# The RMS norm roots of a two-network fp32 kernel: tokens on partitions, one-column sums, and a root spread by TensorE

## What is computed

```
def rmsnorm(x, g):
    return x * rsqrt(mean(x*x, axis=-1) + 1e-6) * g

# network 1, for each of 2 layers; x is 512 tokens x 1024
h = rmsnorm(x, norm_mix_pre)
... h @ w_in: pooling, gated convolution, dilated attention, merged by gates
x = x + rmsnorm(merged @ w_out, norm_mix_post)
h = rmsnorm(x, norm_mem_pre)
x = x + rmsnorm(memory_cross_attention(h, rmsnorm(mem), ...), norm_mem_post)
h = rmsnorm(x, norm_ffn_pre)
x = x + rmsnorm(ffn(h), norm_ffn_post)

# network 2, for each of 2 layers; 512 tokens and, in layer 0, 256 context tokens
h = modulate(rms_norm(x, g), shift, scale)
x = x + gate * rms_norm(mixer(h) @ w_out, g)
h = modulate(rms_norm(x, g), shift, scale)
x = x + gate * rms_norm(mlp(h), g)
```

## Time and profile before

| | |
|---|---|
| time, median of 3 runs | 3810.55 us (3807.89 to 3810.62) |
| span of the profiled execution | 3805.3 us, 5.2 us less than that median, which is what lies around the span |
| PE busy, DVE busy, ACT busy, POOL busy | 95%, 53%, 40%, 6% of the span |
| the chain that ended last | PE 82%, DVE 8%, ACT 6%, issue 2% |
| ACT_TABLE_LOAD of line 1366 | 26, 33.4 us in all |

### The profile page before, as it was taken

One profiled execution on the slowest core, in us unless ns is written; L12 is line 12 of the kernel. 1 busy time (PEld: TensorE's weight loads), 2 busy tenths in 40 slices (PEclk: granted clock), 3 DMA queues, 4 the chain that ended last, 5 costly groups with the idle time before them and its releaser, 6 DMA issues.

```text
span 3805.3 us, 52598 instructions
## 1 busy us (share of the span) xinstructions
PE 3605.1 (95%) x19348; PEld 2957.6 (78%) x19348; DVE 2018.6 (53%) x3396; ACT 1504.8 (40%) x2302; POOL 241.7 (6%) x384
## 2 busy tenths in 40 slices
PE   8999989999999998899999988899999998899998
PEld 6788876887787887688778776788888777667886
DVE  4634466777764455577774465442333444644344
ACT  4344354332324534533235366432122334743233
POOL 0000000001000000000000052000000002610000
PEclk9999999999999999999999999999999999999999
DMA  3222322446332233144551102111211122112322
GB/s 132 93 72 95 98 80 83 147 140 195 119 99 78 71 106 108 42 149 139 191 164 56 50 2 42 45 50 61 66 61 61 55 63 58 31 45 78 99 94 83
DMA packets 113071, 333.14 MB, mean 88 GB/s; under 512 B 32792, under 2 KB 33688, under 8 KB 112408
## 3 DMA queue, kind: packets, MB, share of 16 engines
q1 hardware_dynamic: 74112, 265.23, 21.6%
q0 software_dynamic: 14400, 52.44, 4.3%
q10 hardware_dynamic: 24408, 13.46, 1.6%
HBM read 328.99 MB, written 6.00 MB: 88 GB/s over the span
## 4 chain that ended last, share of the span: by engine, by line
PE 82%; DVE 8%; ACT 6%; issue 2%; DVEq 1%; POOL 0%; ACTq 0%; DMA 0%; POOLq 0%; SPq 0%
PE PS L602 14%; PE PS L604 13%; PE PS L603 13%; PE PS L984 10%; PE PS L985 10%; PE PS L987 10%; PE PS L1112 1%; PE PS L677 1%; PE PS L771 1%; ACT PB L1675 1%; ACT FULL_P L1675 1%; ACT L1366 1%; PE PS L783 1%; DVE HVAL L1958 1%; DVE Y L2371 1%
## 5 line engine op out<-in xcount | busy, mean ns | idle before, releaser
L1914 DVE TENSOR_TENSOR WL<-RAW,WH 128x1024 fp32r<-128x1024 f32 x494 | 604.5, 1224 | 573.5 <-ACT WH L1330 568.2
L1330 ACT ACTIVATE WH<-RAW 128x1024 fp32r<-128x1024 f32 x494 | 521.2, 1055 | 636.3 <-PE PS L987 350.2
L602 PE MATMUL PS<-HHI,WH 128*128 128x512 f32 x1632 | 651.2, 399 | 24.5 <-DVE HLO L1951 16.2
L604 PE MATMUL PS<-HHI,WL 128*128 128x512 f32 x1632 | 639.9, 392 | 0.0
L603 PE MATMUL PS<-HLO,WH 128*128 128x512 f32 x1632 | 638.0, 391 | 0.0
L984 PE MATMUL PS<-H2HI,WH 128*128 128x512 f32 (+1 forms) x1336 | 470.0, 352 | 0.0
L985 PE MATMUL PS<-H2LO,WH 128*128 128x512 f32 (+1 forms) x1336 | 446.6, 351 | 0.0
L602 PEld LDWEIGHTS PS<-HHI,WH 128*128 128x128 f32 x1632 | 307.4, 188 | 105.3 <-issue 19.7
L987 PE MATMUL PS<-H2HI,WL 128*128 128x512 f32 (+1 forms) x1336 | 387.4, 350 | 0.0
L604 PEld LDWEIGHTS PS<-HHI,WL 128*128 128x128 f32 x1632 | 307.1, 188 | 70.5
L603 PEld LDWEIGHTS PS<-HLO,WH 128*128 128x128 f32 x1632 | 307.3, 188 | 64.3 <-issue 0.5
(11 more groups left out here) (353 smaller groups left out, 5737.0 us busy)
## 6 DMA issues: line engine op xcount, KB each, us to landing
RAW<-in_stream SPq DMA_DIRECT2D x494, 512.0 KB, 3.6
MODW<-in_modw POOLq DMA_DIRECT2D x96, 512.0 KB, 4.6
bias_rows<-in_rpb ACTq DMA_DIRECT2D x8, 476.2 KB, 6.7
X<-in_x SPq DMA_DIRECT2D x4, 512.0 KB, 5.5
MEM<-in_mem ACTq DMA_DIRECT2D x2, 1024.0 KB, 4.9
CROW<-in_crow POOLq DMA_DIRECT2D x4, 512.0 KB, 4.7
BIAS<-bias_rows ACTq DMA_DIRECT2D x8, 224.0 KB, 5.0
GRID<-bias_rows ACTq DMA_DIRECT2D x8, 224.0 KB, 4.6
```

The costliest lines, as they stand in the source:

```text
L602: nc.tensor.matmul(out, WH[:, slot, b * P:(b + 1) * P], hi, start=start, stop=False)
L604: return nc.tensor.matmul(out, WL[:, slot, b * P:(b + 1) * P], hi, start=False, stop=stop)
L1330: A(WH[:, d, :], RAW[:, s, :], ACT.Copy).then_inc(high_split, 1)
L1914: TT(WL[:, d, :], RAW[:, s, :], WH[:, d, :].bitcast(F32), ALU.subtract).then_inc(split_ready, 1)
```

## The change

RS moves from SBUF to PSUM banks 6 and 7. The sums are taken with the roles of the operands turned: a 128 x 128 block of the squares is the stationary matrix and one column of ones the moving one (`token_sums`), so a set of 512 tokens is four matmuls of one column, and the sums of 128 tokens come to lie on 128 partitions, 4 or 6 columns in all (TOKEN_SUMS, in bank 5). ACT takes a square root of 128 x 4 or 128 x 6 (ROOT), DVE its reciprocal (ROOT_INVERSE), and TensorE multiplies that column, repeated 128 times as the stationary matrix, by the identity (`roots_spread`), which puts the root of each token on all partitions of RS. Four matmuls of `keep_clock` go ahead of these. `statistics` sums ACC with seven squares in it and then the eighth square by itself. The last `split_high` and `split_low` of a stage move behind the square root and behind the residual. In ACT's evictions the square comes before the copy, and its end is signalled by itself. The table of the square root is loaded ahead of the squares. `keep_clock` writes bank 2 and not 5, and the identity is brought in by ACT's queue at the start. The diff, cut to its core:

```diff
@@ -123,6 +123,8 @@
+        ROOT = place("ROOT", [P, 8])
+        ROOT_INVERSE = place("ROOT_INVERSE", [P, 8])
...
@@ -137,7 +139,6 @@
-        RS = place("RS", [P, TA], at=S0 + 3 * TA)
...
@@ -254,6 +255,8 @@
+        RS = FLAT[:, 6 * T:6 * T + TA]
+        TOKEN_SUMS = FLAT[:, 5 * T + TC:5 * T + TC + 8]
...
@@ -472,7 +475,6 @@
-            sp.dma_start(IDENT[:], consts[:, 0:P]).then_inc(consts_in, 16)
...
@@ -654,17 +656,38 @@
-                    nc.tensor.matmul(bank(5, P), ONES[:], IDENT[:], start=True, stop=True)
-
-            def statistics(n):
+                    nc.tensor.matmul(bank(2, P), ONES[:], IDENT[:], start=True, stop=True)
+
+            def token_sums(src, n, start, stop):
+
+                for b in range(n // P):
+                    last = nc.tensor.matmul(TOKEN_SUMS[:, b:b + 1], src[:, b * P:(b + 1) * P], ONES[:, 0:1], start=start and b == 0, stop=stop,
+                                            skip_group_check=True)
+                return last
+
+            def roots_spread(n):
+
+                keep_clock(4)
+                m.add("inverted")
+                pe.wait_ge(root_inverted, m.at("inverted"))
+                for b in range(n // P):
+                    last = nc.tensor.matmul(RS[:, b * P:(b + 1) * P], ROOT_INVERSE[:, b:b + 1].to_broadcast([P, P]), IDENT[:], start=True, stop=True,
+                                            skip_group_check=True)
+                last.then_inc(root_ready, 1)
+
+            def statistics(n, last_square=None):
...
-                m.add("sqt", KB - 1)
+                m.add("sqt", KB - 2)
...
-                for c0 in range(0, n, T):
-                    c1 = min(c0 + T, n)
-                    last = nc.tensor.matmul(FLAT[:, 6 * T + c0:6 * T + c1], ONES[:], ACC[:, c0:c1], start=True, stop=True)
-                last.then_inc(stat_done, 1)
+                token_sums(ACC[:], n, True, False)
+                if last_square is None:
+                    m.add("sq", KB)
+                    pe.wait_ge(sq_ready, m.at("sq"))
+                else:
+                    pe.wait_ge(y_squared, last_square)
+                token_sums(SQ[:, 1, :], n, False, True).then_inc(stat_done, 1)
+                roots_spread(n)
...
@@ -672,11 +695,8 @@
-                    for c0 in range(0, n, T):
-                        c1 = min(c0 + T, n)
-                        last = nc.tensor.matmul(FLAT[:, 6 * T + c0:6 * T + c1], ONES[:], SQ[:, k % 2, c0:c1], start=k == 0, stop=k == KB - 1,
-                                                skip_group_check=True)
-                    last.then_inc(sq_summed, 1)
+                    token_sums(SQ[:, k % 2, :], n, k == 0, k == KB - 1).then_inc(sq_summed, 1)
+                roots_spread(n)
...
@@ -1306,7 +1324,7 @@
-                statistics(TA if full else T)
+                statistics(TA if full else T, (l + 1) * KB)
...
@@ -1365,21 +1383,22 @@

-            def root(n, dst=None, src=None, summed=False):
+            def root(n, summed=False):
                 if summed:
...
                     act.wait_ge(stat_done, m.at("stat"))
-                inverse_root(RS[:, 0:n] if dst is None else dst, FLAT[:, 6 * T:6 * T + n] if src is None else src).then_inc(root_ready, 1)
+                A(ROOT[:, 0:n // P], TOKEN_SUMS[:, 0:n // P], ACT.Sqrt, bias=COL[:, 0:1]).then_inc(root_taken, 1)

...
                 m.add(f"use{p}")
-                A(Y[:, k, :], bank(3 * p), ACT.Copy)
-                A(dst[:, 0:n], bank(3 * p), ACT.Square, scale=D ** -0.5).then_inc(taken[p], 1)
-                split_high()
+                A(dst[:, 0:n], bank(3 * p), ACT.Square, scale=D ** -0.5).then_inc(sq_ready, 1)
+                A(Y[:, k, :], bank(3 * p), ACT.Copy).then_inc(taken[p], 1)
+                if k < KB - 1:
+                    split_high()

...
@@ -1546,12 +1566,12 @@
+                act.preload_act_table(ACT.Sqrt)
...
-                act.preload_act_table(ACT.Ln)
...
+                split_high()
...
-                act.preload_act_table(ACT.Ln)
...
@@ -1572,17 +1592,18 @@
                     p = (m.n["units"] - 1) % SLOTS
-                    A(Y[:, k, :], bank(3 * p + k % 2), ACT.Copy)
-                    sq = A(dst[:, 0:n], bank(3 * p + k % 2), ACT.Square, scale=D ** -0.5)
-                    sq.then_inc(taken[p] if k % 2 else sq_ready, 1)
+                    A(dst[:, 0:n], bank(3 * p + k % 2), ACT.Square, scale=D ** -0.5).then_inc(sq_ready, 1)
+                    copied = A(Y[:, k, :], bank(3 * p + k % 2), ACT.Copy)
                     if k % 2:
-                        split_high()
-
+                        copied.then_inc(taken[p], 1)
+                        if k < KB - 1:
+                            split_high()
+
+                act.preload_act_table(ACT.Sqrt)
                 squares(of_mo, T)
-                act.preload_act_table(ACT.Ln)
                 root(T)
+                split_high()
                 squares_summed(of_x, T)
-                act.preload_act_table(ACT.Ln)
                 root(T, summed=True)
...
@@ -1849,15 +1867,16 @@
                     m.add(f"use{p}")
-                    A(Y2[:, k, 0:n], FLAT[:, 3 * p * T:3 * p * T + n], ACT.Copy)
-                    A(dst[:, 0:n], FLAT[:, 3 * p * T:3 * p * T + n], ACT.Square, scale=D ** -0.5).then_inc(taken[p], 1)
-                    split_high()
+                    A(dst[:, 0:n], FLAT[:, 3 * p * T:3 * p * T + n], ACT.Square, scale=D ** -0.5).then_inc(sq_ready, 1)
+                    A(Y2[:, k, 0:n], FLAT[:, 3 * p * T:3 * p * T + n], ACT.Copy).then_inc(taken[p], 1)
+                    if k < KB - 1:
+                        split_high()

                 n2 = TA if full else T
-                act.preload_act_table(ACT.Ln)
+                act.preload_act_table(ACT.Sqrt)
                 squares(of_y2, n2)
                 root(n2)
-                act.preload_act_table(ACT.Ln)
+                split_high()
                 squares_x(full, False)
...
@@ -1882,18 +1901,18 @@
+                act.preload_act_table(ACT.Sqrt)
...
-                    split_high()
+                    if k < KB - 1:
+                        split_high()
...
-                m.add("sqt", KB - 1)
-                act.preload_act_table(ACT.Ln)
+                m.add("sqt", KB - 2)
...
-                if l == 0:
-                    act.preload_act_table(ACT.Ln)
+                split_high()
...
@@ -1923,6 +1942,8 @@
+                if k == KB - 1:
+                    return
...
@@ -1936,11 +1957,14 @@
                     m.add(f"use{j % 2}")
-                for p in range(2) if k == 1 else (k % 2,):
-                    dve.wait_ge(taken[p], m.at(f"use{p}", 1))
-
-            def root_inverse(n):
+                sq_arrived(k)
+
+            def root_inverse(n, meanwhile=None):
                 m.add("root")
+                dve.wait_ge(root_taken, m.at("root"))
+                nc.vector.reciprocal(ROOT_INVERSE[:, 0:n // P], ROOT[:, 0:n // P]).then_inc(root_inverted, 1)
+                if meanwhile is not None:
+                    meanwhile()
                 dve.wait_ge(root_ready, m.at("root"))
...
@@ -2207,6 +2231,7 @@
+                    split_low()
...
@@ -2214,8 +2239,9 @@
                     add_squares(k, T, y_arrived)
-                    split_low()
-                root_inverse(T)
+                    if k < KB - 1:
+                        split_low()
+                root_inverse(T, split_low)

...
```

More of the change, by code:

```diff
@@ L457, in build @@
         RAW_LAPS = tuple(f"lap{s}" for s in range(RAW_SLOTS))
-        MARKS = ("sum", "of", "qkh", "qks", "vh", "vs", "r", "sc", "comb", "ptl", "modw0", "modw1", "crow", "modu", "relu", "y", "hsq", "bias", "in2", "units", "use0", "use1", "consts", "mem", "pool", "x", "sq", "sqt", "stat", "root", "val", "hi", "lo", "pooled", "mixed",
+        MARKS = ("sum", "of", "qkh", "qks", "vh", "vs", "r", "sc", "comb", "ptl", "modw0", "modw1", "crow", "modu", "relu", "y", "hsq", "bias", "in2", "units", "use0", "use1", "consts", "mem", "pool", "x", "sq", "sqt", "stat", "root", "inverted", "val", "hi", "lo", "pooled", "mixed",
                  "vt", "vtr", "roped", "s", "max", "exp", "pt", "pts", "o", "otk", "merge", "gate", "ab", "conv", "silu", "otd", "inverse", "sums", "w") + RAW_LAPS
@@ L717, in memory_sums @@
                     nc.tensor.matmul(FLAT[:, 6 * T:6 * T + TC], ONES[:], MEM_SQ[:, k, :], start=k == 0, stop=k == KB - 1).then_inc(sq_summed, 1)
-            pe.wait_ge(ones_in, 32)
+            pe.wait_ge(ones_in, 48)
             sum_squares(T, 0)
-            pe.wait_ge(consts_in, 16 * 5)
+            pe.wait_ge(consts_in, 16 * 4)
             for l in range(DEPTH):
@@ L899, in _ @@
                 statistics(T)
-                m.add("sq", KB)
                 m.add("max", 16)
@@ L1432, in memory_root @@
                 inverse_root(MR[:], FLAT[:, 6 * T:6 * T + TC]).then_inc(mr_ready, 1)
-            act.preload_act_table(ACT.Ln)
-            act.wait_ge(ones_in, 32)
```

(23 more changed lines are left out.)

8 lines of the change are left out of this document (2 added, 6 removed).

## The result

The changed kernel takes 3878.63 us (median of 4 runs, 3876.48 to 3879.98) against 3809.63 us (3807.89 to 3810.62) for the kernel before in the same comparison. The ratio is 1.0183, 95% interval 1.0170 to 1.0195. It is 69 us slower, where 18.6 us less had been forecast, and it lies far outside the range. The profiled execution of it has a span of 3874.6 us. Further on, one execution of e6 (8108.83 us) and one of the kernel before in the same comparison (12554.62 us) are left out as slow ones.

What follows compares the result with a forecast made beforehand. TensorE, with 82% of the span, was taken to bound the kernel, the norms leaving it idle. Terms 5.0 + 2.55 + 11.65 - 0.6 = 18.6 us took the span from 3805.3 to 3786.7, forecast 3792 us, range 3777 to 3811.

Steps and rivals of the forecast that it cites:

- most of the kernel is products and this change touches none of them: Whole kernel: 82% of the span is on TensorE, mostly products; the change can touch only the norms.
- the price of one-column sums in a norm of x: Sums of squares on TensorE: 0.109 us a record, 0.87 us a set of 512 tokens, 1.31 of 768.
- the handshake of 2.16 us: Each norm, from the last sums to VectorE's first use of the root: 3.06 us becomes 2.16 on 512 tokens.
- the one-column sums can't keep up: Rival, norms of x: at 0.19 us a record TensorE sets the pace; net 19 us slower, 3830; chance 0.11.
- a gain of 7.55 in the forecast: Eight norms of x: 5.0 us from five on 512 tokens plus 2.55 from three on 768.
- A cheap column: Rival, all sums: a one-column record costs 0.061 us, saving 13.7 us more, 3778; chance 0.24.
- the upper row: One-column record price: upper bound from the `keep_clock` record, same weights and 128 moving columns, 0.122 us; 0.109 taken.
- Norms of a result: Twelve `statistics` norms: shorter TensorE list and handshake gain 11.65 us, the first norm after mixing counting nothing.
- 0.6 had been taken: Tables, evictions, splits: 0.6 us lost to table loads ahead of the paired attention of network 2.
- The pair behind a norm: Products behind a norm: VectorE's list, not `keep_clock(16)`, sets their end, so the gain stays; otherwise 10.8 us lost.

Runs made afterwards that it cites:

- e6: e5 without the four `keep_clock` matmuls ahead of the spread of the root; 3793.41 us, ratio 0.9960 to the kernel before.
- e1: The kernel before with 16 unused words (64 bytes) per partition where ROOT and ROOT_INVERSE lie in the changed kernel; 3843.86 us against 3809.16, ratio 1.0092.
- e2: The changed kernel with ROOT and ROOT_INVERSE placed in scratch that RS left, so nothing else moves; 3846.51 us, ratio 1.0095 to the kernel before.
- e5: e3 with 128 columns of ones in the norms of x on 768 tokens too; 3794.11 us against 3808.43 for the kernel before.
- e12: e5 with the last high and low splits back ahead of square root and reciprocal; 3795.25 us, ratio 0.9965 to the kernel before.
- e8: The kernel before with 16 unused words ahead of the weights, so weights and activations move by 64 bytes together; 3807.41 us, ratio 0.9997.
- e3: e2 with token sums moving 128 columns of ones (64 for 768 tokens) instead of one; 3806.03 us against 3809.16 for the kernel before.

## Why the prediction was wrong

*What failed first had no term at all.* The prediction says that "most of the kernel is products and this change touches none of them". It does touch them, by its first two lines, which place two small tensors. In the diff they read as nothing, and in the order of instructions nothing shows. The step of a product went from 0.2289 to 0.2324 us. e1 puts the price at 34.7 us by 64 bytes alone, e2 gets 32 back. This term stood at nothing in the sum. No rival had it, so even the slowest, 3830, fell short of 3878.

*The second step that failed was the price of one-column sums in a norm of x.* The 0.109 us a record was right where the clock is full (0.89 us a set after memory attention), and so was the handshake of 2.16 us (2.19 there). What failed was the step that took the clock to be full through the sums. The rival "the one-column sums can't keep up" had the mechanism: granted clock 0.50, TensorE the pace of the norm. It was given 0.11. Its size for a norm on 512 tokens was close, 2.8 us worked out and 2.7 to 4.0 measured; for 768 tokens 3.3 had been taken and 5.5 to 8.0 were measured. The record took 0.213 us, not 0.19: the 0.19 came from counting the records that touch 2 us in the earlier trace rows, and the steps in that same trace are 0.213 too. In all the eight norms lost 36.1 us, against the rival's 24 and a gain of 7.55 in the forecast. What spoke against it, that `keep_clock` was back at 0.117 us a record by 612.67, was read wrongly: it showed that 512-column sums bring the clock back in the course of the norm, as the stretches of the earlier trace rows together say, and not that the opening 18 matmuls keep it. The one-column sums didn't bring it back: in the changed kernel it stayed at 0.50 from 613.3 until they ended at 622.75, and in a norm on 768 tokens for 16.5 us of them (3087.9 to 3104.4).

*A cheap column*, given 0.24, was wrong at either clock: 8 records in 0.89 us, 0.111 each. The median step at the full clock is 0.112 us with one, 64 or 128 moving columns, and 0.213 at half of it with each of them. So the upper row was the right one, and the prediction read it a little high: 1.95 us over 16 records holds the tail of the last, and their step is 0.112 and not 0.122. The Trainium skill, "TensorE: Matmul & The Clock Gate", section "LDWEIGHTS (loading the stationary operand)", has columns / 1.2 ns, 107 ns. The 0.112 us agree with it within 5%, the 0.213 at half the clock don't.

*Norms of a result.* The term of 11.65 us was right. In e5, where the tensors lie as in the kernel before, the twelve gain 11.9 us from the first `keep_clock` matmul to VectorE's first use. That the sum fits so well is partly luck: the norms after mixing gained 0.3 and 0.6 where nothing was counted. After the FFN 2.24 was taken twice from one place, where the handshake of the kernel before ran at a granted clock of 0.50; there 2.4 was measured, and 1.3 in layer 1, where that clock had been 1.00.

*What is left of the 18.6.* With sums of 128 columns and the tensors left alone the change brings 14.3 us (e5). Its eight norms of x gain 5.4 and not 7.55: four gain 0.9 each, as good as the 1.0 forecast, but the first and two of those on 768 tokens gain only 0.1 to 0.5. Between the norms its trace gives back 4.3 us where 0.6 had been taken; where, was not traced. The mean granted clock of e5 is 0.993 against 0.986 before, so a part of its gain is clock, and the two were not told apart. The last low part brings nothing by its move behind the root (e12).

*The pair behind a norm.* "I count the gain as kept" was right ahead of the FFN. In e5 HVAL is 3.82 us early there. The first product, at 615.04, is only 2.97 us early, as worked out (3.13 us behind HVAL where it was 2.28 in the earlier trace rows). From the ninth product on they are 3.84 us early, so the start of the pair didn't matter. Behind the first norm of network 2's layer 1 it did not hold fully: there the pair gives 1.3 us back.

## What to carry to other kernels

A profile's "busy" doesn't say whether TensorE keeps its clock: here it was busy for 9.45 of 9.45 us at a granted clock of 0.50. Look at the granted clock and at the step between records. When wide matmuls are replaced by narrow ones ahead of a critical stretch, check the clock there first; the cheapest remedy to try is the same instruction with more moving columns, which cost nothing here, 0.112 us a record with one or with 128.

A tensor that is placed ahead of others is a change to every part of the kernel that reads them. Put new ones behind the others or in freed space, and compare the step of an untouched product in both traces before explaining anything else. And try a few places of the moving operand against the weights once, since each costs a line.

## What the runs showed of the hardware

A product of 128x128 weights with 512 columns took 0.2267, 0.2289, 0.2324 or 0.2333 us, by the place of the moving operand in SBUF against the weights within 256 bytes (0, 64, 128, 192), and the same 0.2289 when both moved together (e8). Why it does so no run here tells.

At the granted clock of 0.50 the step between records with 128 weight columns was 0.213 us, and at 1.00 it was 0.112, with one, 64 or 128 moving columns alike. The clock stayed at 0.50 through 9.4 and 16.5 us of one-column sums in the changed kernel and through 15.9 and 11.8 us of 64-column ones in e3. With 128 columns it stayed at 1.00 through the same norms (e5). With 64 columns it also stayed at 1.00 in one norm of x out of three, the first of network 2 (e3), and no run tells what set that one apart.
